# Feed-forward input blocks with both parts of u in one 512-column matmul, the halves added by VectorE

## What is computed

```python
def rms_norm(x, g):
    return x * lax.rsqrt(jnp.mean(x * x, axis=-1, keepdims=True) + RMS_EPS) * g

def swiglu(x, w_in, w_out):
    a, b = jnp.split(x @ w_in, 2, axis=-1)
    return (jax.nn.silu(a) * b) @ w_out

h = x + 0.5 * swiglu(rms_norm(x, ffn1_norm), ffn1_w_in, ffn1_w_out)
...                                   # mixers, gates, output projection
h = h + 0.5 * swiglu(rms_norm(h, ffn2_norm), ffn2_w_in, ffn2_w_out)
```

## Time and profile before

| | us |
|---|---|
| median of 3 runs | 1284.81 (1284.32 to 1286.12) |
| the profiled execution | 1283.03 |
| its span | 1281.1 |

### The profile page before, as it was taken

How to read it: one execution, slowest core, us unless ns; L and a number is a source line. 1 busy time by engine, 2 the same in 40 slices (tenths; PEclk the granted TensorE clock), 3 DMA queues, 4 the chain that set the end, 5 groups by cost and what they waited for, 6 DMA issues and landing times.

```text
span 1281.1 us, 25591 instructions
## 1 busy us (share of the span) xinstructions
PE 1243.2 (97%) x10328; PEld 1220.3 (95%) x10328; DVE 899.9 (70%) x1168; ACT 636.3 (50%) x900; POOL 335.7 (26%) x462
## 2 busy tenths in 40 slices
PE   5999999999889999999999999999998999999998
PEld 5999999899889999999999999998987999999998
DVE  4757757887876876555676677687877778755554
ACT  5654545683544454444456445557635435534432
POOL 0288800344402400000005895004434042000000
PEclk9999999999989999999999999999999999999999
DMA  7555454533334565554545545544333345555551
GB/s 300 198 175 185 168 193 165 198 132 132 114 117 165 170 238 200 186 196 173 188 136 200 190 168 197 192 165 165 132 132 132 131 166 202 193 192 172 188 172 65
DMA packets 31029, 220.46 MB, mean 172 GB/s; under 512 B 3568, under 2 KB 3568, under 8 KB 4592
## 3 DMA queue, kind: packets, MB, share of 16 engines
q1 hardware_dynamic: 30960, 219.49, 48.6%
HBM read 218.42 MB, written 1.05 MB: 171 GB/s over the span
## 4 chain that ended last, share of the span: by engine, by line
PE 84%; DVE 8%; POOL 5%; ACT 2%; issue 1%; DMA 0%; SPq 0%; DVEq 0%; ACTq 0%
PE banks L456 27%; PE banks L458 27%; PE banks L457 27%; PE banks L469 3%; DVE w_lo_t L1081 3%; POOL st L1643 1%; POOL s5x L1641 1%; DVE s5x L1285 1%; ACT w_hi_t L820 1%; POOL st L1646 1%; POOL s5x L1640 1%; POOL st L1644 1%; DVE u_lo_t L1095 1%; POOL st L1548 1%; DVE hT L1234 1%
## 5 line engine op out<-in xcount | busy, mean ns | idle before, releaser
L1081 DVE TENSOR_TENSOR w_lo_t<-raw,w_hi_t 128x1024 fp32r<-128x1024 f32 x404 | 517.3, 1320 | 113.2 <-ACT w_hi_t L820 112.9
L820 ACT ACTIVATE w_hi_t<-raw 128x1024 fp32r<-128x1024 f32 x404 | 403.3, 1046 | 141.7 <-PE banks L458 141.2
L456 PE MATMUL banks<-u_hi_t,w_hi_t 128*128 128x256 f32 x1520 | 437.6, 288 | 14.7 <-DVE w_lo_t L1081 14.3
L457 PE MATMUL banks<-u_lo_t,w_hi_t 128*128 128x256 f32 x1520 | 433.5, 285 | 0.0
L458 PE MATMUL banks<-u_hi_t,w_lo_t 128*128 128x256 f32 x1520 | 433.3, 285 | 0.0
L456 PEld LDWEIGHTS banks<-u_hi_t,w_hi_t 128*128 128x128 f32 x1520 | 295.2, 194 | 20.3 <-DVE w_lo_t L1081 14.3
L457 PEld LDWEIGHTS banks<-u_lo_t,w_hi_t 128*128 128x128 f32 x1520 | 295.5, 194 | 0.1
L458 PEld LDWEIGHTS banks<-u_hi_t,w_lo_t 128*128 128x128 f32 x1520 | 295.2, 194 | 0.0
L456 PE MATMUL banks<-b_hi_t,w_hi_t 128*128 128x256 f32 x864 | 244.9, 283 | 0.0
L458 PE MATMUL banks<-b_hi_t,w_lo_t 128*128 128x256 f32 x864 | 244.5, 283 | 0.0
L457 PE MATMUL banks<-b_lo_t,w_hi_t 128*128 128x256 f32 x864 | 244.5, 283 | 0.0
(11 more groups left out here) (215 smaller groups left out, 1268.5 us busy)
## 6 DMA issues: line engine op xcount, KB each, us to landing
raw<-weights SPq DMA_DIRECT2D x203, 1024.0 KB, 4.9
prm<-params SPq DMA_DIRECT2D x1, 1178.5 KB, 5.5
prm<-params SPq DMA_DIRECT2D x1, 1166.5 KB, 15.1
cst<-constants SPq DMA_DIRECT2D x1, 1027.0 KB, 11.2
hT<-x_t SPq DMA_DIRECT2D x2, 512.0 KB, 5.7
raw<-weights SPq DMA_DIRECT2D x2, 512.0 KB, 6.5
out_t<-hT SPq DMA_DIRECT2D x4, 256.0 KB, 2.2
prm<-params SPq DMA_DIRECT2D x1, 12.0 KB, 1.7
```

The lines of the kernel that those rows point to most:

```text
L456: pe.matmul(o, st[0], mv[0], start=start, stop=False, skip_group_check=True)
L457: pe.matmul(o, st[0], mv[1], start=False, stop=False, skip_group_check=True)
L820: act.activation(w_hi[:, slot, a:a + HALF], raw[:, slot, a:a + HALF], ACT.Copy) \
L1081: dve.tensor_tensor(w_lo[:, slot, a:a + HALF], raw[:, slot, a:a + HALF], w_hi[:, slot, a:a + HALF].bitcast(F32), ALU.subtract) \
```

## The change

An input block from the fifth on (j = 4 to 21, 18 in each half step) is issued by a new function, `wide_block`. For each of its 16 weight tiles it has two matmuls: w_hi with u_hi and u_lo side by side (512 columns, a whole bank: w_hi·u_hi in the left half, w_hi·u_lo in the right), and w_lo with u_hi (256 columns, added to the left half). For this u_hi and u_lo lie in one tile `u_t` (and `b_hi`, `b_lo` in `b_t`), with the parts 8 KB apart. Such a block has two PSUM banks, one for a and one for b, so that even tiles have banks 4 and 5, odd ones 6 and 7. ScalarE gets a copy of both right halves to SBUF (`second_half`), VectorE adds the left halves to it and then multiplies by `rstd_row` (`add_and_scale`, two instructions in place of one). The tiles 2 and 3 keep the old form and move to banks 6 and 7. A SiLU on one column (`early`) stands at the head of ScalarE's loop.

```diff
@@ engine TensorE
+                def wide_block(b, slot, bank, where):
+                    block_ready(b)
+                    for kt in range(KT):
+                        for ct in range(2):
+                            st = w(slot, kt * 256 + ct * P, P)
+                            pe.matmul(banks[:, bank + ct, :], st[0], in_t[where][:, :, kt, :],
+                                      start=kt == 0, stop=False, skip_group_check=True)
+                            ins = pe.matmul(banks[:, bank + ct, 0:T], st[1], in_hi[where][:, kt, :],
+                                            start=False, stop=kt == KT - 1, skip_group_check=True)
+                    ins.then_inc(s.w_used, 1)
...
-                            in_block(b0 + 3 * i - 1, (b0 + 2) % 3, 4, where=f)
+                            wide_block(b0 + 3 * i - 1, (b0 + 2) % 3, 4, f)
                         out_block(0 if first else i - 1, b0 + 3 * i, b0 % 3, False)
-                        pe.wait_ge(s.h_ab, layer * PER.h_ab + FT * f + 2 * i)
-                        in_block(b0 + 3 * i + 1, (b0 + 1) % 3, 5, where=f)
+                        if first:
+                            pe.wait_ge(s.row_read, layer * PER.row_read + 2 * f + 1)
+                            in_block(b0 + 4, (b0 + 1) % 3, 7, where=f)
+                        else:
+                            pe.wait_ge(s.h_ab, layer * PER.h_ab + FT * f + 2 * i)
+                            wide_block(b0 + 3 * i + 1, (b0 + 1) % 3, 6, f)
@@ engine ScalarE
+                def second_half(f, j, buf, k, slot):
+                    act.wait_ge(s.w_used, layer * PER.w_used + RING * k + slot + 1 + RING)
+                    act.wait_ge(s.h_prod, layer * PER.h_prod + FT * f + j - 1)
+                    act.activation(ab[:, buf, :, :], banks[:, 4 + 2 * buf:6 + 2 * buf, T:2 * T], ACT.Copy) \
+                        .then_inc(s.h_corr, 1)
...
+                        if not first:
+                            second_half(f, 2 * i, 0, k0 + i - 1, 2)
                         silu(f, 2 * i, 0)
...
                         round_weights(layer, k0 + i + 1, 0)
+                        if not first:
+                            second_half(f, 2 * i + 1, 1, k0 + i, 1)
                         silu(f, 2 * i + 1, 1)
...
                     with act.Fori(2, FT // 2 - 1) as i:
+                        act.activation(early[:, :], one_c, ACT.Silu)
                         body(i)
@@ engine VectorE
+                def add_and_scale(f, j, buf, k, slot):
+                    dve.wait_ge(s.w_used, layer * PER.w_used + RING * k + slot + 1 + RING)
+                    dve.wait_ge(s.h_corr, layer * PER.h_corr + (FT - 4) * f + j - 3)
+                    both = banks[:, 4 + 2 * buf:6 + 2 * buf, :].rearrange("p c (n t) -> p c n t", n=2)
+                    dve.tensor_tensor(ab[:, buf, :, :], both[:, :, 0, :], ab[:, buf, :, :], ALU.add).then_inc(s.h_raw, 1)
+                    dve.wait_ge(s.h_raw, layer * PER.h_raw + (FT - 4) * f + j - 3)
+                    dve.tensor_tensor(ab[:, buf, :, :], ab[:, buf, :, :],
+                                      rstd_row[:, :].unsqueeze(1).to_broadcast([P, 2, T]), ALU.mult).then_inc(s.h_ab, 1)
```

More of the change, by code:

```diff
@@ L108 @@
     w_used = PER_LAYER
+    h_corr = 2 * (FT - 4)
+    h_raw = 2 * (FT - 4)
     h_ab = 2 * FT
@@ L274, in build @@
         ab, hf = sbqk, yb[:, :, 0, :]
-        tiles8 = lambda x: x.rearrange("p n k t -> p (n k) t")
-        in_hi = [u_hi[:, :, :], tiles8(b_hi[:, :, :, :])]
-        in_lo = [u_lo[:, :, :], tiles8(b_lo[:, :, :, :])]
+        u_hi, u_lo = u_t[:, 0, :, :], u_t[:, 1, :, :]
+        b_hi, b_lo = (b_t[:, i, :, :].rearrange("p (n k) t -> p n k t", n=4) for i in range(2))
+        in_t = [u_t, b_t]
+        in_hi = [x[:, 0, :, :] for x in in_t]
+        in_lo = [x[:, 1, :, :] for x in in_t]
         end_hi = [x[:, 6:8, :] for x in (in_hi[1], in_hi[0])]
@@ L304, in build @@
         s.w_used = sem("w_used")
+        s.h_corr = sem("h_corr")
+        s.h_raw = sem("h_raw")
         s.h_ab = sem("h_ab")
@@ L877, in ffn, with body @@
                         act.activation(s5n[:, 0, :], p_("log_step"), ACT.Exp).then_inc(s.s5_exp, 1)
-                    def body(i):
+                    def body(i, first=False):
+                        if not first:
+                            second_half(f, 2 * i, 0, k0 + i - 1, 2)
                         silu(f, 2 * i, 0)
@@ L1203, in ffn, with body @@
                         reduce_angles()
-                    def body(i, bank=4):
-                        scale(f, 2 * i, 0, k0 + i - 1, 2, bank)
+                    def body(i, first=False):
+                        if first:
+                            scale(f, 2 * i, 0, k0 + i - 1, 2, 6)
+                        else:
+                            add_and_scale(f, 2 * i, 0, k0 + i - 1, 2)
                         product(f, 2 * i, 0)
@@ L1210, in body @@
                         rest_of_weights(layer, k0 + i + 1, 0)
-                        scale(f, 2 * i + 1, 1, k0 + i, 1)
+                        if first:
+                            scale(f, 2 * i + 1, 1, k0 + i, 1, 7)
+                        else:
+                            add_and_scale(f, 2 * i + 1, 1, k0 + i, 1)
                         product(f, 2 * i + 1, 1)
@@ L1214, in body @@
                         rest_of_weights(layer, k0 + i + 1, 1)
-                    body(1, bank=6)
+                    body(1, True)
                     with dve.Fori(2, FT // 2 - 1) as i:
@@ L1219, in ffn @@
                     i = FT // 2 - 1
-                    scale(f, FT - 2, 0, k0 + i - 1, 2)
+                    add_and_scale(f, FT - 2, 0, k0 + i - 1, 2)
                     product(f, FT - 2, 0)
@@ L1223, in ffn @@
                     hidden_lo(f, FT - 2, 0, end_hi[f], end_lo[f])
-                    scale(f, FT - 1, 1, k0 + i, 0)
+                    add_and_scale(f, FT - 1, 1, k0 + i, 0)
                     product(f, FT - 1, 1)
```

15 lines of the change are left out of this document (8 added, 7 removed).

## The result

| | median, us | lowest to highest | runs |
|---|---|---|---|
| before | 1284.76 | 1282.91 to 1286.12 | 8 |
| the changed kernel | 1289.74 | 1288.61 to 1292.49 | 8 |

The ratio is 1.0043, with a 95% interval of 1.0031 to 1.0055: slower by 5 us, where 23 us less were forecast. The profiled execution took 1292.26 us, 2.5 more than the median; its span is 1290.5.

A forecast was written before the change was run, and what follows sets the result against it. TensorE was taken to bound the kernel; 28.2 us gained less 5 of lateness gave 23.2 off the profiled 1283.03, so 1259.8, and with the median 1.78 above, 1261.6 us; range 1251 to 1276.

The forecast's parts named there:

- What bounds the kernel: Feed-forward loop: TensorE is busy for the whole 17.28 us round, so each nanosecond it saves comes off the time.
- The price of a 512-column float32r matmul: Wide blocks on TensorE: 216 ns with the weight load hidden, gaining 24.5 ns at each of 1152 places, 28.2 us.
- Rival 1: TensorE stream: the 13 ns belong to each matmul, 512 columns take 227 ns, gain 15.4 us, time 1273.4; chance 20%.
- Rival 3: TensorE stream: only columns count, 512 take 240 ns, no gain, 3 to 5 us lost, time 1289; chance 8%.
- Rival 2: TensorE stream: the load gets cheaper too, 216 + 112 ns, gain 37 us, lateness 6, time 1253.8; chance 9%.
- Rival 4: First half steps: VectorE bounds six or seven GpSimd-busy rounds, each late by 2 us, 26 us, time 1283; chance 7%.
- Lateness beside GpSimd: Tightest rounds of first half steps: the longer VectorE chain delays output blocks 2.5 us each, 5 in all, bounds 1.8 to 12.
- the multiplication: VectorE's new instruction with two SBUF inputs: 0.69 us, stretched by 0 to 0.6 us beside GpSimd in the tightest round.
- ScalarE, PSUM, quiet rounds: Copies of 617 ns fit ScalarE, PSUM bank reuse is far off, the quiet chain keeps 1.2 us in hand: no cost.

The follow-up runs named there:

- the changed kernel without tables: The changed kernel with GpSimd's S5 rotation tables cut to one column a step: 1277.62 us, ratio 0.9953.
- the order in twos: Wide blocks in the second half steps only, each four matmuls ordered 512, 512, 256, 256, against the kernel before: 1277.04 us, ratio 0.9941.
- spread steps: The changed kernel with GpSimd's twelve largest table steps held apart, each waiting for one more tile's product: 1280.30 us, ratio 0.9974.
- both repairs: The changed kernel with matmuls ordered 512, 512, 256, 256 and GpSimd's large table steps held apart, ending one tile earlier: 1276.32 us, ratio 0.9934.

## Why the prediction was wrong

**What bounds the kernel:** right. In quiet rounds TensorE is still busy throughout, and where the stream got shorter by 2.13 us, the half step did.

**The price of a 512-column float32r matmul: the step that failed.** The prediction reads the 13 ns beside the columns as a weight load that is longer than 107 ns, takes the 3 ns of plain float32 instead, and so has 216 ns. Alone it takes 227, the rival's number, and in turn with 256 columns 236. Of 24.5 ns a place 11 go with the fee (227 for 216) and 7 with the turns; 6.7 are left. By the half steps, 2.13 us / 288 places, it is 7.4. So the gain is 8.5 us where 28.2 were forecast. Two things in the reasoning failed: that plain float32 can stand for float32r, and that the load makes the 120 ns and hides 107 ns of columns. A float32r matmul of 192 columns with its load takes 112. The rows had 120 against half of 216 in them, 13 ns for the one pass and 2.5 for two; the lowest price consistent with both was taken for the likeliest.

**The rivals.** Rival 1, the fee, has its mechanism, though without the turns and with too little lateness: 1273.4. Rival 3 gave 1289 and a deciding point at a spacing of 236 ns; the time came out at its number and the spacing at its point, yet its mechanism, a rate of columns, falls by 384 columns at 173.5 ns. A hit of a number is no evidence here. Rival 2, a cheaper load, is seen at most in the 117 ns of the 256-column matmul, more than paid for by the 236 before it. Rival 4 did not come: one long wait in the loop of each first half step, in the place forecast, not six.

**Lateness beside GpSimd: right in place and mechanism, too small.** Forecast 2.5 us a first half step, bounds 0.9 to 6; measured 6.8 and 6.9. (The prediction's own working ends at 3.7 us late; nothing in it gives the 6.) Of that the chain alone is 3.4. The term mis-sized is the multiplication, costed at 0 to 0.6 us of stretch from a mean over rows; it is 1.5, and the product behind it is stretched by 0.6, which the sum had at nothing. Then TensorE arrives earlier at the same wait by more than the 0.39 us of one block that the sum had (1.0), and the clock falls at the wait, which it had not (2.3).

**ScalarE, PSUM, quiet rounds:** right. The copy takes 0.60 where 0.62 was put, the one-column SiLU costs nothing that can be seen, the chain in quiet rounds stays hidden, and TensorE never waits in the second half steps.

**The sum as measured:** 4 x 2.13 gained, 6.8 + 6.9 lost: 5.2 us slower, against 5.0 between the medians.

**What stays open:** where in TensorE the 13 ns of float32r arise, and why a change of column count costs 6.6 ns; the 15.9 at 448 columns; when the clock falls at a wait. And the mixers: by the ratios the changed kernel without tables gains 6.0 us where its half steps gain 8.5, the wide blocks without the addition 4.8 of 5.6, and the wide blocks in the second half steps 3.9 of 4.3, or 7.6 of 6.7 with the order in twos. What sets this was not tried. With spread steps it is 3.3 of 7.4, and with both repairs 8.5 of 10.3, and there most of it is in sight: the waits for `u_t` at the step to the mixers are 2.7 and 1.7 us.

## What to carry to other kernels

Price a matmul of a new width from rows of its own type, and put a stream of it alone on the chip before rewriting around it; two matmuls merged into one save one fee and nothing of the columns, and half of the fee went again where the stream then changed between two widths (6.6 of 13.3 ns). An instruction that is moved from a PSUM input to two SBUF inputs becomes open to GpSimd's large steps: it ended only behind the one that ran at its start. So look in the tightest round at what GpSimd has beside it, not at a mean. Where a gain upstream ends in a wait downstream, the wait grows by that gain, and the clock may fall at it besides: cure the chain first.

## What the runs showed of the hardware

- A float32r matmul with 256 to 512 columns has 13 ns beside its columns; plain float32 and bf16 have 2.5. With 128 and 192 columns it takes 112 ns.
- Matmuls of 512 and 256 columns in turn cost 353.3 ns a pair, in twos 348.4, while separate runs of each add up to 346.7. In bf16 the turns cost nothing (325.0).
- VectorE's 128x512 multiplication out of SBUF took 2.17 us beside GpSimd's 1024-column steps and 0.69 without them; the addition with an input in PSUM 0.68 and 0.69. Each stretched multiplication ended 0.55 us behind the GpSimd instruction that ran at its start, each stretched 128x256 product or hidden_lo 0.28 us behind it.
- At waits of TensorE of 4.0 us between full blocks the granted clock was 0.50 for 6.8 us, at waits of 2.9 us (512 and 256 columns in twos) and at one of 2.2 us for 3.4 us; at 3.1 and 3.3 us behind blocks of 256-column matmuls, and at others of 2.2 and 2.7 us behind wide blocks, it stayed at 1.00.
